# Two weight pieces of branch C's merge gate move into the loading ring among the modulation's pieces

## What is computed

```python
def modulate_project(x, mod, w_in):
    shift, scale, gate = jnp.split(mod, 3, axis=-1)
    u = (layer_norm(x) * (1.0 + scale) + shift).astype(x.dtype)
    return split_columns(u @ w_in), gate

def merge_residual(x, ys, zs, g_merge, gate, w_branch, w_out, ln_g, ln_b, alpha):
    gates = jnp.split(jax.nn.sigmoid(g_merge), N_BRANCH, axis=-1)
    merged = sum(gb * ((yb * jax.nn.silu(zb)) @ w_branch[i])
                 for i, (yb, zb, gb) in enumerate(zip(ys, zs, gates)))
    h = alpha * x + gate * (merged @ w_out)
    return (layer_norm(h) * ln_g + ln_b).astype(x.dtype)

# mod, for the context and for the latents: silu(c) @ w_mod[l] + b_mod[l]
```

## Time and profile before

| | |
|---|---|
| median of 3 runs | 1567.56 us (1567.0 to 1567.74) |
| the profiled execution's own time | 1569.26 us |
| its span, first to last instruction | 1567.5 us |
| PE busy | 1518.7 us (97% of the span) |
| DVE, ACT, POOL busy | 740.1, 474.7, 627.8 us (47%, 30%, 40%) |
| mean granted clock of TensorE | 0.998 of full speed |

### The profile page before, as it was taken

How to read it: one execution, slowest core, us unless ns; L and a number is a source line. 1 busy time by engine, 2 the same in 40 slices (tenths; PEclk the granted TensorE clock), 3 DMA queues, 4 the chain that set the end, 5 groups by cost and what they waited for, 6 DMA issues and landing times.

```text
span 1567.5 us, 22612 instructions
## 1 busy us (share of the span) xinstructions
PE 1518.7 (97%) x9079; PEld 1247.1 (80%) x9079; DVE 740.1 (47%) x1447; ACT 474.7 (30%) x1099; POOL 627.8 (40%) x500
## 2 busy tenths in 40 slices
PE   5999999999999999999999999999989999999997
PEld 4898788886688887788878877889758888778886
DVE  4496710656523342722497584125580236152257
ACT  1146710156410123411144475012571003232010
POOL 2561045700355454145773400555004553423562
PEclk9999999999999999999999999999999999999999
DMA  9220012317222222125430200222301222211521
GB/s 350 86 85 28 1 54 81 95 62 245 76 67 81 64 72 58 31 71 184 126 122 29 68 15 14 68 81 81 125 15 54 78 70 68 67 48 41 175 81 68
DMA packets 76281, 128.72 MB, mean 82 GB/s; under 512 B 16205, under 2 KB 20753, under 8 KB 76177
## 3 DMA queue, kind: packets, MB, share of 16 engines
q1 hardware_dynamic: 73936, 121.24, 25.1%
q10 hardware_dynamic: 2240, 6.03, 1.1%
HBM read 120.96 MB, written 6.30 MB: 81 GB/s over the span
## 4 chain that ended last, share of the span: by engine, by line
PE 81%; DVE 8%; POOL 3%; issue 3%; ACT 2%; DMA 1%; SPq 0%; POOLq 0%; DVEq 0%; ACTq 0%
PE pb L1006 55%; PE pb L1150 5%; PE pb L1279 4%; PE pb L1031 3%; PE pb L1230 2%; PE pb L1193 2%; PE pb L954 2%; PE pb L1201 1%; PE pb L1460 1%; PE pb L1323 1%; DVE ks L2103 1%; DMA stage<-in_w_mod 1%; ACT pr L1743 1%; DVE nm L2244 1%; POOL slot_T L848 1%
## 5 line engine op out<-in xcount | busy, mean ns | idle before, releaser
L1006 PE MATMUL pb<-wsp,act_T 128*128 128x512 f32 x3048 | 712.3, 391 | 3.1 <-POOL wsp L848 1.2
L1006 PEld LDWEIGHTS pb<-wsp,act_T 128*128 128x128 f32 x3048 | 568.3, 188 | 126.4 <-issue 8.4
L845 POOL CAST wsp<-raw 128x1024 fp32r<-128x1024 f32 x128 | 136.7, 1068 | 813.5 <-PE pb L1006 598.4
L848 POOL TENSOR_TENSOR wsp<-raw,wsp 128x512 fp32r<-128x512 f32 x268 | 359.6, 1363 | 10.2
L1006 PE MATMUL pb<-wsp,yT 128*128 128x512 f32 x720 | 165.7, 389 | 0.0
L1006 PEld LDWEIGHTS pb<-wsp,yT 128*128 128x128 f32 x720 | 135.0, 188 | 27.9
L2573 DVE SCALAR_TENSOR_TENSOR mt<-tg,pb 128x512 f32<-128x512 f32 x40 | 27.4, 685 | 216.6 <-PE pb L1006 215.8
L1893 ACT ACTIVATE tg<-pb 128x512 f32<-128x512 f32 x60 | 35.9, 599 | 275.9 <-PE pb L1006 275.9
L1743 ACT ACTIVATE pr<-pb,nm 128x640 f32<-128x640 f32 (+2 forms) x128 | 91.3, 713 | 4.8 <-DVE nm L2244 4.8
L1230 PE MATMUL pb<-ident,pr 128*128 128x128 f32 x480 | 73.9, 275 | 4.4 <-ACT pT L1778 3.7
L2573 DVE SCALAR_TENSOR_TENSOR merged<-tg,pb 128x512 f32<-128x512 f32 x20 | 13.8, 688 | 119.9 <-PE pb L1006 119.9
(11 more groups left out here) (295 smaller groups left out, 1957.0 us busy)
## 6 DMA issues: line engine op xcount, KB each, us to landing
raw<-in_w_in SPq DMA_DIRECT2D x112, 512.0 KB, 3.6
raw<-in_w_mod SPq DMA_DIRECT2D x32, 512.0 KB, 4.6
raw<-in_w_branch SPq DMA_DIRECT2D x24, 512.0 KB, 3.7
raw<-in_w_out SPq DMA_DIRECT2D x16, 512.0 KB, 3.6
stage<-in_w_mod SPq DMA_DIRECT2D x12, 512.0 KB, 11.6
raw<-in_w_in SPq DMA_DIRECT2D x16, 256.0 KB, 5.1
xh<-in_x_sample SPq DMA_DIRECT2D x6, 512.0 KB, 6.6
out<-xh ACTq DMA_DIRECT2D x5, 512.0 KB, 2.9
```

The source lines that it names most:

```text
L845: pool.tensor_copy(hi, raw[:, p % 3, :, 0:width]).then_inc(raw_hi, 1)
L848: ins = pool.tensor_tensor(lo[:, j, :], raw[:, p % 3, j, 0:width], hi[:, j, :].bitcast(F32), ALU.subtract)
L1006: mm = pe.matmul(dst, lhs(a, k, t), w[:, wa, j, 0:width], start=(k == 0 and n == 0), stop=(i == count - 1 and j == 1 and n == 2))
```

## The change

It places G0 in the list right before the second modulation chunk of the layer (after m0 to m3), and G1 right after that chunk (after m4 to m7). G2 and G3 stay behind the last modulation piece. POOL's wait for the last probability is removed: it splits both pieces when they have landed. The new table `at` gives PE the list positions of a product's pieces, since they no longer stand together. PE's instructions keep their order; their waits name another of the three ring semaphores in places.

```diff
-    def add(self, layer, key, matrix, blocks, *columns, slots=None, of=None, by_act=False, last=T - 1):
-        self.first[layer, key] = len(self.items)
+    def add(self, layer, key, matrix, blocks, *columns, slots=None, of=None, by_act=False, last=T - 1,
+            part=None):
+
+        self.first.setdefault((layer, key), len(self.items))
         self.chunk[key] = blocks // 2
-        for i, k in enumerate(range(0, blocks, 2)):
+        part = range(blocks // 2) if part is None else part
+        for i in part:
+            k = 2 * i
             p = len(self.items)
+            self.at.setdefault((layer, key), []).append(p)
...
-                for ll, c in LATE_CHUNKS[l]:
+
+                for n, (ll, c) in enumerate(LATE_CHUNKS[l]):
+                    if n == 1:
+                        add((br, "G", 0), "in", KD, (COL_G + BRANCH[br] * D, HALF), part=(0,))
                     add(("gmod", ll, c), "mod", KD, (c * HALF, HALF), of=ll)
+                    if n == 1:
+                        add((br, "G", 0), "in", KD, (COL_G + BRANCH[br] * D, HALF), part=(1,))
...
-            add((br, "G", hf), "in", KD, (COL_G + i * D + hf * HALF, HALF))
+            add((br, "G", hf), "in", KD, (COL_G + i * D + hf * HALF, HALF),
+                part=(2, 3) if (br, hf) == ("C", 0) else None)
...
-            def split_late(p, l):
-
-                g = pieces.first[l, ("C", "G", 0)]
-                if p == g + 1:
-
-                    pool.wait_ge(p_ready[l], NL + 1 + NL)
-                split(p)
-
...
                 if z[3] < p < pieces.first[1, ("kv",)]:
-                    split_late(p, 0)
+                    split(p)
...
-                        p = first + i
+                        p = at[i]
```

More of the change, by code:

```diff
@@ L113, in __init__ @@
         self.first = {}
+        self.at = {}
         self.chunk = {}
@@ L146, in add @@
             self.items.append((matrix, layer if of is None else of, k, columns))
-        if matrix != "mod":
+        if matrix != "mod" and part[-1] == blocks // 2 - 1:
             self.last[len(self.items) - 1] = (layer, (*key, last))
@@ L929, in _ @@
                 if p > z[3]:
-                    split_late(p, 1)
+                    split(p)
             for t in range(T):
@@ L987, in product @@
                             after=None):
-                    first, count = pieces.first[here[0], chunk], pieces.chunk[chunk]
+                    at, count = pieces.at[here[0], chunk], pieces.chunk[chunk]
                     part = range(count) if part is None else part
```

## The result

| | before | changed |
|---|---|---|
| median | 1567.65 us (4 runs, 1567.0 to 1568.79) | 1577.89 us (4 runs, 1575.67 to 1580.6) |
| ratio, 95% interval | | 1.0064 (1.0052 to 1.0075) |
| profiled execution, its span | 1569.26, 1567.5 us | 1580.6, 1578.8 us |

The account below looks back on a forecast made before the run. PE was taken as the bound, on four fifths of the chain. Late m6 5.2 + 4.8, clock 1.6 + 1.6, gains -2.75 - 0.3 gave +10.2 us on the median 1567.56: 1577.7 us, range 1572.0 to 1582.5 (8 in 10).

Parts of the forecast that it names:

- The late m6: Attention, both layers: m6 must wait for G0's load and split in its ring place; +5.2 us layer 0, +4.8 layer 1.
- the gain: Moving G0's split from behind the modulation pieces gives back 2.75 us in layer 0; moving layer 1's split gives 0.3 us.
- the clock's price: PE's idling ahead of m6 brings one 3.4 us stretch at half clock behind it; +1.6 us in each layer.
- crowding: Layer 0, m10 behind G1's load and split: counted as 0, up to 2 us if the loads crowd.
- G0's split in the ring: Between PE's uses of m1 and m6: G0's load and split delay m6 by 5.2 us (layer 0), 4.8 (layer 1).
- The 1.0 us for the stores: After m1's release, two stores take 0.98 us of SP's queue before G0's load is issued.
- the trip: From m1's release to m6's landing: stores, G0's load, its split, m6's load, one after another; 13.4 us.
- The ring's next turn: Layer 0 behind m6: m8's 0.6 us overlaps the clock's cost; G1's split holding m10 costs 0, up to 2 us.
- the second rival: The ring stays behind: missed places are not made up, +12.2 to +15.4 us, 1579.8 to 1583.0 us; chance 0.12.
- The removed hold: End of the attention, both layers: nobody waits for G1 or its split there, so ending its hold gives 0.
- The Trainium skill's estimate: About 2.0 us fixed plus bytes at 436 GB/s: 3.2 us per 512 KB load, giving +5.8 us, 1573.3 us.

Follow-up runs that it names:

- e5: Changed kernel with one of two subtractions left out in the splits of G0 and G1, both layers; 1574.08 us, ratio 1.0043 to the kernel before.
- e6: The change made in layer 1 alone, layer 0 as in the kernel before; 1572.08 us, ratio 1.0029 to the kernel before.
- e3: Kernel before, with G0 held as well as G1 until the attention's last probability is normalised; 1564.49 us, ratio 0.9977 to the kernel before.
- e1: Changed kernel with G0 and G1 loaded into a fourth buffer beside the ring, order unchanged; 1571.68 us, ratio 1.0026 to the kernel before.
- e2: Changed kernel with only G0 among the modulation pieces, G1 behind them and held as before; 1575.93 us, ratio 1.0049 to the kernel before.
- e4: Kernel before with only the hold removed, so G1 is split right behind G0; 1574.07 us, ratio 1.0038 to the kernel before.
- e8: Changed kernel, G0 and G1 in a buffer beside the ring, only half of each loaded and split; 1566.39 us, ratio 0.9987 to the kernel before.

## Why the prediction was right, step by step

The forecast was 1577.7 us and the measured median 1577.89. The mechanism is the one predicted, but the sum met the median better than its terms met the profiled execution, and that is in part luck: the rows of both layers add up to +11.7 us where the sum had +10.2. The late m6 was put 1.5 us too high in the two layers and the gain 1.2 us too low; the clock's price in the rows was 0.4 us too low, and 3.9 us of crowding stood at 0.

- **G0's split in the ring.** Forecast +5.2 and +4.8 us at m6. From m0 to m6 the rows give 15.3 instead of 10.6 us in layer 0, +4.7, and 14.8 instead of 11.0 in layer 1, +3.8. The chain of load, split and load is there link by link. The 1.0 us for the stores was wrong: SP issues them while it waits for m1's release (second store at 345.36, release by 346.1), so they are in front of the trip and not in it. The first load took 5.1 and 4.7 us, not 4.6; the split 3.7 and the second load 4.0 us, as taken.
- **The clock.** Forecast +1.6 us in each layer; measured +1.3 behind m6 in layer 0 and +2.3 in layer 1, where the slow stretch was twice as long. That there would be a slow stretch behind each large wait was read from one case, and it is no rule: e5 had waits of 1.9, 1.7 and 2.2 us in layer 0 and none. The changed kernel's four executions have a mean clock of 0.994 to 0.998, and only the one with 0.994 was profiled; how much of the clock's price the other three paid is open.
- **The ring's next turn.** Taken as 0, with up to 2 us if loads crowd. In the profiled execution they crowd: PE waits 2.08 us at m10, and a second slow stretch follows. The delay since m0 is 6.0 us at m8 and 9.9 at m11, +3.9. This is the second rival in layer 0 of this one execution (1580.6 us, within that rival's range); layer 1 has no m10 and no second slow stretch, and the other three executions are in the forecast's range. That layer 0 costs 5.8 us over all runs (changed less e6), where the profiled one shows 6.6, fits an execution somewhat worse than most.
- **The gain.** Forecast -2.75 and -0.3. Layer 0 gave back 12.38 - 9.08 = 3.3 us. The prediction took layer 1's 9.63 us for what remains without a split, but these steps have waits of their own there, and e3 shows 9.08 for layer 0. Layer 1 gave back 1.0 us, since the delay is 6.1 us at m7 and 5.1 at the gate product. e3 measures the whole gain alone: -3.2 us in the medians, near the forecast's 3.05, and 4.7 in the rows of the profiled executions (3.2 and 1.5), of which that of before was 1.6 us above its median.
- **The removed hold.** Taken as 0, and right for the place where the hold ended: the changed kernel, which has no split there, and e3, which has two, both keep the 0.9 us wait for `ytmp` in layer 1. That the hold protected 6 us where G1 stood was not seen.
- **The cause of the waits.** The prediction charged the delay to the ring place alone and left bytes to the second rival. The runs divide it: of the 13.4 us between the changed kernel and e3, 6.2 go with the ring place (e1) and 7.2 stay with the loads among the modulation pieces. The parts overlap in the changed kernel, where the added loads lengthen a trip that PE waits for anyway, so they are not two terms that the sum could have kept apart by its rows.
- **The Trainium skill's estimate** (DMA: Bandwidth & Descriptors, Anatomy of one DMA; a fit for DMAs issued through GpSimd) of 3.2 us for a 512 KB load would have given 1573.3 us. The trip's loads, issued by SP, took 4.0 to 5.1 us, and the measurement decides for the rows.

In layer 1 G0's load was foreseen at about 1117 us and is issued at 1121.83, because the prediction did not shift layer 1 by what layer 0 loses. Nothing in the sum hangs on it.

How the 7.2 us of e1 over e3 divide can be read from their rows: from m0 to the gate product e1 is 3.9 and 3.6 us longer. PE's waits for DMAs are 4.0 us in layer 0 and 2.0 in layer 1, and the slow stretch of layer 1 costs 1.3 more. Only 0.2 us is left for the splits and all else. What stays open is why the clock falls behind some waits of 2 us and not behind others, and how the waits grow with the bytes.

## What to carry to other kernels

In a ring that one queue fills in order, a piece holds its place from its issue to its release, and the piece that comes next in that place must be loaded after that. What this trip takes beyond the consumer's own work in the meantime is lost: here 12.9 us against 8.2 in layer 0, 4.7 us. Ask who frees the place and who waits for the piece that comes three later, and leave pieces with a slow consumer outside the stretch where a fast consumer empties the ring as soon as it is filled. Look also at the room in the loads themselves: where each landing is used at once, moved bytes can cost time even with a buffer of their own (e1). And when an engine beside the path disturbs one on it, holding its work back to a place with cover (e3) can win more than spreading it.

## What was not expected of the hardware

- The time at the lower clock varied: 3.4 us in each slow stretch of layer 0, before the change and after it, but 6.8 us in layer 0 of e2 and, from about 1133.3 to 1140.1, in layer 1 of the changed kernel, though there PE had been busy without a break since 1134.19.
- The same wait does not always have the same effect on the clock: it fell to 0.50 behind 1.54 us (before), 1.68 (e6) and 2.04 us (e1, layer 1) and stayed at 1.00 behind 2.09 us (e1, layer 0) and 2.23 us (e5).
- Two splits in a row beside the softmax cost more than twice one: G0's alone costs 3.2 us over both layers (before less e3), G1's right behind it 6.4 us more (e4 less before).
- A load of 512 KB more cost about 2 us of wait in three places of four (e1), and one of 256 KB 0.5 and 0.7 us in two of four and nothing in the others (e8).
- The executions of the changed kernel spread over 4.9 us, those of e3 over 0.9 us. That loads which just miss, and the clock behind them, make the time vary is a guess; only one execution of each kernel was profiled.
